# A two-block transformer kernel: another order for the last layers' products and weight splits, and a value projection that moves high and low weights together

## The reference, cut to what matters

```python
proj = xn @ w_in[layer]
sb_q, sb_k, sb_v, r_q, r_k, r_v, r_g = jnp.split(proj, split_at, axis=-1)
```

```python
hm = rmsnorm(x, norm_mlp_g[l])
x = x + jnp.square(jax.nn.relu(hm @ w_up[l])) @ w_down[l]
return rmsnorm(x, norm_final_g)
```

## Time and profile before

| what | value |
|---|---|
| median of 3 runs | 1605.78 us |
| profiled execution | 1605.47 us |
| its span in the trace | 1603.7 us |
| PE busy | 1565.6 us (98%) |
| DVE busy | 983.5 us (61%) |
| ACT busy | 789.0 us (49%) |
| POOL busy | 608.2 us (38%) |
| granted clock of PE, mean | 0.99 |

### The profile page before, as it was taken

How to read it: one execution, slowest core, us unless ns; L and a number is a source line. 1 busy time by engine, 2 the same in 40 slices (tenths; PEclk the granted TensorE clock), 3 DMA queues, 4 the chain that set the end, 5 groups by cost and what they waited for, 6 DMA issues and landing times.

```text
span 1603.7 us, 20315 instructions
## 1 busy us (share of the span) xinstructions
PE 1565.6 (98%) x7628; PEld 1275.3 (80%) x7628; DVE 983.5 (61%) x1217; ACT 789.0 (49%) x925; POOL 608.2 (38%) x245
## 2 busy tenths in 40 slices
PE   9999999999999999999999999999999989898988
PEld 7888888688888888888898688668868868787876
DVE  6366211782465899899875699744434664737374
ACT  5365222334345788878863432964244533333334
POOL 1422454134342232222225555444314445362725
PEclk9999999999999999999999999999999999999998
DMA  5421243222246999999964336002402323050511
GB/s 203 125 73 53 79 145 118 79 79 80 103 149 238 385 419 405 393 390 390 383 246 143 105 104 173 31 27 79 150 35 79 132 80 130 4 206 1 184 40 53
DMA packets 49768, 252.18 MB, mean 157 GB/s; under 512 B 9953, under 2 KB 12769, under 8 KB 23457
## 3 DMA queue, kind: packets, MB, share of 16 engines
q1 hardware_dynamic: 43344, 238.42, 40.4%
q0 software_dynamic: 5184, 8.40, 1.4%
q10 hardware_dynamic: 1168, 4.39, 0.7%
HBM read 235.57 MB, written 16.78 MB: 157 GB/s over the span
## 4 chain that ended last, share of the span: by engine, by line
PE 82%; DVE 6%; ACT 5%; issue 5%; POOL 2%; DMA 1%; POOLq 0%; SPq 0%; DVEq 0%; ACTq 0%
PE psum L232 23%; PE psum L234 23%; PE psum L233 23%; PE psum L2379 2%; ACT unit_hi L2792 1%; ACT f_hi L2864 1%; PE psum L2414 1%; PE psum L1350 1%; PE psum L1072 1%; PE psum L2402 1%; PE psum L2672 1%; POOL w_lo L148 1%; ACT w_hi L142 1%; POOL unit_lo L2797 1%; DVE f_relu L2940 1%
## 5 line engine op out<-in xcount | busy, mean ns | idle before, releaser
L148 POOL TENSOR_TENSOR w_lo<-raw,w_hi 128x2048 fp32r<-128x2048 f32 x62 | 285.5, 4606 | 470.3 <-ACT w_hi L142 435.4
L1368 DVE TENSOR_TENSOR moe_lo<-moe_w,moe_hi 128x2048 fp32r<-128x2048 f32 x100 | 228.3, 2292 | 31.4 <-ACT moe_hi L1358 30.1
L232 PE MATMUL psum<-x_hi,w_hi 128*128 128x512 f32 (+1 forms) x624 | 241.9, 388 | 1.0 <-POOL w_lo L148 1.0
L233 PE MATMUL psum<-x_lo,w_hi 128*128 128x512 f32 (+1 forms) x624 | 239.6, 384 | 0.0
L234 PE MATMUL psum<-x_hi,w_lo 128*128 128x512 f32 (+1 forms) x624 | 239.6, 384 | 0.0
L142 ACT ACTIVATE w_hi<-raw 128x2048 fp32r<-128x2048 f32 x67 | 128.0, 1911 | 208.3 <-PE psum L234 207.8
L2797 POOL TENSOR_TENSOR unit_lo<-mlp_raw,unit_hi 128x2048 fp32r<-128x2048 f32 x32 | 155.3, 4852 | 168.6 <-DVE unit_lo L2797 88.9
L1358 ACT ACTIVATE moe_hi<-moe_w 128x2048 fp32r<-128x2048 f32 x100 | 191.4, 1915 | 28.0 <-PE psum L234 21.6
L232 PEld LDWEIGHTS psum<-x_hi,w_hi 128*128 128x128 f32 x624 | 117.3, 188 | 26.0 <-issue 3.0
L233 PEld LDWEIGHTS psum<-x_lo,w_hi 128*128 128x128 f32 x624 | 117.3, 188 | 23.4 <-issue 0.7
L234 PEld LDWEIGHTS psum<-x_hi,w_lo 128*128 128x128 f32 x624 | 117.2, 188 | 23.1
(11 more groups left out here) (422 smaller groups left out, 3397.3 us busy)
## 6 DMA issues: line engine op xcount, KB each, us to landing
raw<-in_w_dense SPq DMA_DIRECT2D x67, 1024.0 KB, 4.9
...
```

Of the source, the lines that this page charges most:

```text
L148: pool.tensor_tensor(w_lo[c % RING][:, :], raw[c % RING][:, :], w_hi[c % RING][:, :].bitcast(F32), ALU.subtract).then_inc(lo_ready, 1)
L232: pe.matmul(out, lh, rh, start=first, stop=False, **more)
L233: pe.matmul(out, lh, rl, start=False, stop=False, **more)
L1368: dve.tensor_tensor(ring_lo[s][:, :], ring[s][:, :], ring_hi[s % MOE_HI][:, :].bitcast(F32), ALU.subtract).then_inc(moe_low, 1)
```

## The change

It touches two places.

In the value projection, the high and the low weights now lie in one tensor `w_both`, at the same addresses. One step is two matmuls instead of three: `x_hi` against the high and the low weights side by side in 512 columns, and `x_lo` against the high weights in 256 columns, added to the left half. The two halves of the bank are added by VectorE when it reads them (a TENSOR_REDUCE over 512 elements in place of a copy of 256).

In the last layer pair:
- VectorE lowers units 0, 2 and 3 (before: 2 and 3), so GpSimd lowers one unit less in each group.
- Products 2 to 5 are A12, S4, S2, S3 (before: S2, A12, S3, S4), with other banks, raw quarters, add order and rows to match. `weights_1` stands after pair c = 1 (group 0: c = 0), behind the lowering of unit 0. `weights_2` and the lowering of units 2 and 3 follow `parts_low` of c = 3. `weights_3` and `weights_4` follow the first adds.
- ScalarE rounds a pair's combinations (`parts_high`) before the weight unit that stood ahead of it, save in c = 3. In group 0 the rounding of up0's last chunk (`split_hi` of UP0_C + 3) now stands behind `parts_high` of c = 1.
- At the end, rows q = 2, 3 are squared, gained and scaled first.

```diff
-            for kt in range(KT):
-                mm = three_pass(pe, psum[:, 6 if j in SECOND_V else 7, 0:2 * P], x_hi[:, kt, m * P:(m + 1) * P], x_lo[:, kt, m * P:(m + 1) * P],
-                                wh[:, :, kt, :], wl[:, :, kt, :], kt == 0, kt == KT - 1)
+                pe.matmul(psum[:, bank, :], x_hi[:, kt, rows], wb[:, :, :, kt, :], start=kt == 0, stop=kt == KT - 1,
+                          skip_group_check=True)
+                mm = pe.matmul(psum[:, bank, 0:2 * P], x_lo[:, kt, rows], wb[:, 0, :, kt, :], start=False, stop=kt == KT - 1,
+                               skip_group_check=True)
...
-            dve.tensor_copy(ret_v[:, j % 4, 256 * (j // 4):256 * (j // 4) + 256], psum[:, 6 if j in SECOND_V else 7, 0:256])\
-               .then_inc(bank_free, 1)
+            dve.tensor_reduce(ret_v[:, j % 4, 256 * (j // 4):256 * (j // 4) + 256],
+                              psum[:, bank, :].rearrange("p (s n) -> p n s", s=2), AX.X, ALU.add).then_inc(bank_free, 1)
...
-    LOWERED_BY_VECTOR = (2, 3)
+    LOWERED_BY_VECTOR = (0, 2, 3)
...
-        slots.append([a3, a1, a2, a0])
+        slots.append([a2, a3, a1, a0])
...
-    SUM_OF_UNIT = {1: 1, 2: 3, 4: 2, 6: 4}
-    RAW_OF_UNIT = (B11, B11, B11, B21, B12, B22, B11, 0, 1, 2, 3)
+    SUM_OF_UNIT = {1: 1, 4: 2, 5: 3, 6: 4}
+    RAW_OF_UNIT = (B11, B11, B21, B22, B11, B12, B11, 0, 1, 2, 3)
...
                 rectified(g, 2 * c)
-                if c == 2:
-                    weights_1(g)
-                if c == 3:
-                    weights_2(g)
                 rectified(g, 2 * c + 1)
                 sums(g, c)
                 parts_low(g, c)
-                if c == 2:
-                    weights_3(g)
+                if c == (1 if g else 0):
+                    unit_lower(dve, UNITS * g)
+                    weights_1(g)
                 if c == 3:
                     unit_lower(dve, UNITS * g + 2)
+                    weights_2(g)
+                    unit_lower(dve, UNITS * g + 3)
...
-            add(g, 0, BANKS_X, 2, 0, -4)
-            add(g, 1, BANKS_Y, 0, 1, -3)
-            unit_lower(dve, UNITS * g + 3)
-            add(g, 2, BANKS_X, 2, 1, -2)
+            add(g, 1, BANKS_Y, 0, 1, -2)
+            add(g, 0, BANKS_X, 2, 0, -5)
+            add(g, 2, BANKS_Z, 2, 0, 1)
+            weights_3(g)
             weights_4(g)
...
-            product(g, 2, S2, BANKS_X, added=0)
-            product(g, 3, A12, BANKS_Z, begins=True)
-            product(g, 4, S3, BANKS_X, added=2)
-            product(g, 5, S4, BANKS_Y, added=1)
-            product(g, 6, A22, BANKS_X, added=4)
+            product(g, 2, A12, BANKS_Z, begins=True)
+            product(g, 3, S4, BANKS_Y, added=0)
+            product(g, 4, S2, BANKS_X, added=1)
+            product(g, 5, S3, BANKS_X, added=4)
+            product(g, 6, A22, BANKS_X, added=5)
```

More of the change, by code:

```diff
@@ L93, in build @@
     raw = [at(f"raw{b}", 8 * b, [P, CHUNK_COLS]) for b in range(RING)]
-    w_hi = [at(f"w_hi{b}", 16 + 8 * b, [P, CHUNK_COLS], FR) for b in range(RING)]
-    w_lo = [at(f"w_lo{b}", 32 + 8 * b, [P, CHUNK_COLS], FR) for b in range(RING)]
+    w_both = at("w_both", 16, [P, 2, RING, CHUNK_COLS], FR)
+    w_hi, w_lo = ([w_both[:, i, b, :] for b in range(RING)] for i in range(2))
     x_hi = at("x_hi", 48, [P, KT, S], FR)
@@ L693, in ret_v_tile @@
             b, m = j // 4, j % 4
-            wh = w_hi[(V_C + b) % RING][:, :].rearrange("p (m k n) -> p m k n", k=KT, n=P)
-            wl = w_lo[(V_C + b) % RING][:, :].rearrange("p (m k n) -> p m k n", k=KT, n=P)
+            wb = w_both[:, :, (V_C + b) % RING, :].rearrange("p s (m k n) -> p s m k n", k=KT, n=P)
             if m == 0:
@@ L2820, in mlp_sync @@
                 sp.wait_ge(lows_done, ONCE + UNITS * (g - 1) + 4 + k)
[L2821 to L2822 removed]
+                if k < 2:
+                    sp.wait_ge(t_added, ONCE + 4 * (g - 1) + 3 + k)
                 load("up", g, k)
@@ L2837, in mlp_gpsimd @@
         split_lo(pool, UP0_C + 2)
-        unit_lower(pool, 0)
         split_lo(pool, UP0_C + 3)
-        for U in range(1, UNITS * G - 4):
+        for U in range(UNITS * G - 4):
             if U % UNITS not in LOWERED_BY_VECTOR:
@@ L2844, in mlp_gpsimd @@
         pool.wait_ge(gain_landed, ROWS_LANDED + 16)
+        for q in range(2, TB):
+            pool.wait_ge(p_added, done + 7 + q)
+            pool.tensor_tensor(y_rows[q][:, :], res_t[q][:, :], gain_row[:, :], ALU.mult).then_inc(last_gained, 1)
         for q in range(2):
-            pool.wait_ge(p_added, done + 9 + q)
+            pool.wait_ge(p_added, done + 11 + q)
             pool.tensor_tensor(y_rows[q][:, S:D], res_t[q][:, S:D], gain_row[:, S:D], ALU.mult).then_inc(last_gained, 1)
-        for q in range(2, TB):
-            pool.wait_ge(p_added, done + 9 + q)
-            pool.tensor_tensor(y_rows[q][:, :], res_t[q][:, :], gain_row[:, :], ALU.mult).then_inc(last_gained, 1)
     def mlp_scalar(act):
@@ L2873, in mlp_scalar @@
         squares(0, 0)
+        parts_high(0, 0)
         unit_high(act, 0)
-        parts_high(0, 0)
         squares(0, 1)
+        parts_high(0, 1)
         split_hi(act, UP0_C + 3, UP0_T + 4)
-        parts_high(0, 1)
         rows_copied(0)
@@ L2881, in mlp_scalar @@
         squares(0, 2)
+        parts_high(0, 2)
         unit_high(act, 1)
-        parts_high(0, 2)
         rows_copied(2)
@@ L2892, in mlp_scalar @@
                 unit_high(act, U0 - 2)
-                squares(g, 0)
-                unit_high(act, U0 - 1)
-                parts_high(g, 0)
-                for c in range(1, 4):
+                for c in range(3):
                     squares(g, c)
-                    unit_high(act, U0 + c - 1)
                     parts_high(g, c)
+                    unit_high(act, U0 - 1 + c)
+                squares(g, 3)
+                unit_high(act, U0 + 2)
+                parts_high(g, 3)
             for n in range(3, PRODUCTS + 2 * (g + 1 < G)):
@@ L2903, in mlp_scalar @@
         done = 2 * PRODUCTS * (G - 1)
+        for q in range(2, TB):
+            act.wait_ge(p_added, done + 7 + q)
+            act.activation(sq_rows[q % 2][:, :], res_t[q][:, :], ACT.Square, accum_out=row_sum[:, q:q + 1])\
+               .then_inc(last_squared, 1)
+        act.wait_ge(last_squared, COUNTED + 2)
+        act.activation(row_rms[:, 2:TB], row_sum[:, 2:TB], ACT.Sqrt, scale=1.0 / D, bias=col("eps")).then_inc(last_rooted, 1)
         for q in range(2):
-            act.wait_ge(p_added, done + 9 + q)
+            act.wait_ge(p_added, done + 11 + q)
             act.activation(sq_rows[q][:, 0:S], res_t[q][:, S:D], ACT.Square, accum_out=right_sum[:, q:q + 1])\
                .then_inc(last_squared, 1)
+        act.wait_ge(last_inverted, COUNTED + 1)
         for q in range(2, TB):
-            act.wait_ge(p_added, done + 9 + q)
-            act.activation(sq_rows[q % 2][:, :], res_t[q][:, :], ACT.Square, accum_out=row_sum[:, q:q + 1])\
-               .then_inc(last_squared, 1)
-        act.wait_ge(last_squared, COUNTED + TB)
-        act.activation(row_rms[:, 2:TB], row_sum[:, 2:TB], ACT.Sqrt, scale=1.0 / D, bias=col("eps")).then_inc(last_rooted, 1)
-        for q in range(2, TB):
-            act.wait_ge(last_gained, COUNTED + q + 1)
-            act.wait_ge(last_inverted, COUNTED + 1)
+            act.wait_ge(last_gained, COUNTED + q - 1)
             act.activation(y_rows[q][:, :], y_rows[q][:, :], ACT.Copy, scale=row_rstd[:, q:q + 1]).then_inc(last_right, 1)
@@ L3021, in mlp_vector @@
         dve.reciprocal(row_rstd[:, 2:TB], row_rms[:, 2:TB]).then_inc(last_inverted, 1)
+        dve.wait_ge(last_squared, COUNTED + TB)
+        dve.tensor_scalar(right_mean[:, 0:2], right_sum[:, 0:2], 1.0 / D, EPS, ALU.mult, ALU.add).then_inc(last_mean, 1)
         done = 2 * PRODUCTS * (G - 1)
```

26 lines of the change are left out of this document (12 added, 14 removed).

## The result

| | before | after |
|---|---|---|
| median of 4 runs | 1605.43 us | 1582.97 us (1582.57 to 1584.94) |
| profiled execution | 1605.47 us | 1584.94 us |
| its span | 1603.7 us | 1583.1 us |

The ratio is 0.9861, with a 95% interval from 0.9844 to 0.9878. 1582.0 had been forecast, with a range from 1577 to 1589.

A forecast was written before the change was run, and what follows sets the result against it. TensorE, busy 98% of the span, was taken to bound the kernel. Terms of -19.2, -2.3, +0.2, -1.3 and -1.2 sum to -23.8 us: from 1605.47 to 1581.7, with 0.3 for the median 1582.0 us, range 1577 to 1589.

The forecast's parts named there:

- value projection: Value steps: merged matmuls 13.3 ns shorter, -1.7 us over 128 steps; with the longer reading, -1.2 us left.
- group 0, to the start of c = 3: Last layer pair: up0 ends 6.0 us later, c = 3 starts at 1297.9 instead of 1297.68, +0.2 us.
- groups 1 to 3: Last layer pair: stops go, a group takes 82.05 us; 265.34 us between starts of c = 3 becomes 246.15, -19.2 us.
- last 132 matmuls: The 12 of c = 3 and products 2 to 6 at the end: 32.63 us becomes 30.4, -2.3 us.
- the end: After TensorE's end: VectorE's add for q = 1 comes about 0.9 us after it instead of 2.2, -1.3 us.
- The stops ahead of c = 3: TensorE's waits for `f_lo` in each group, about 4.4 us and 2.5 us of lower clock, go in groups 1 to 3.
- T: Moment when TensorE ends the last up tile; `f_lo` of c = 3 forecast at T + 7.0, due at T + 8.16.
- The wait ahead of product 5: Each group: unit 5, lowered by GpSimd, ends at T + 27.6 for T + 27.2, a new wait of 0.45 us.
- The lower clock: Group 0: 2.1 us added for TensorE's slower clock behind the idle ahead of up0's last chunk, which starts 3.9 us late.
- the rivals: Stop stays in part, 1598 us (0.07); slower chain, 1611 (0.05); group 0 and reading cost more, 1588 (0.06); nothing, 1605 (0.02).
- the slower one: Unit 4, `weights_3`, unit 5, product 5: GpSimd slips one pass, product 5 waits 5.1 us, 1611 us; chance 0.05.

The follow-up runs named there:

- the second: The changed kernel once more, unaltered, on one chip beside other kernels: 1583.36 us (1582.03 to 1583.78).
- the last layer pair alone: The changed kernel with the value projection as it was before (three matmuls of 256 columns, a copy): 1585.08 us, ratio 0.9866.
- the early chunk: The changed kernel with up0's last chunk rounded ahead of the high parts of c = 1 in group 0: 1579.49 us, ratio 0.9837; again 1579.46 us.
- the last experiment: The early chunk with the value projection as it was before (three 256-column products, a copy): 1581.31 us against 1579.46.

## Why the prediction was right, and what its terms measured

The spans fell by 20.6 us in the first profile after, by 22.3 in the second. By stretches, in us:

| term | predicted | first profile | second |
|---|---|---|---|
| value projection | -1.2 | -0.5 | -0.5 |
| untouched code ahead of the last pair | 0 | +1.0 | +0.9 |
| group 0, to the start of c = 3 | +0.2 | -0.3 | -1.9 |
| groups 1 to 3 | -19.2 | -18.1 | -18.1 |
| last 132 matmuls | -2.3 | -1.9 | -1.9 |
| the end | -1.3 | -0.8 | -0.8 |
| sum | -23.8 | -20.6 | -22.3 |

Groups 1 to 3 are 1545.18 - 1297.90 = 247.28 us where they were 265.34. Group 0 is counted from the first matmul of up0's third chunk, 1260.65 after and 1260.10 before.

- **The stops ahead of c = 3.** Mechanism and size were right: no idle, clock 1.00, `f_lo` at T + 7.1 for T + 7.0. Undoing a part of the new order brings stops back: 1.1 us for `f_lo` with unit 0 on GpSimd, 3.2 us for unit 1 with `weights_1` late. No run shows how much of the old stop each of the two combinations made.
- **The wait ahead of product 5.** Predicted 0.45 us, measured 0.47 to 0.57. The term was short by 0.3 us a group: the interval to the matmul behind the stop is 0.87 us (1399.10 to 1399.97) and to the next 0.34, so the stop costs 0.87 + 0.34 - 2 x 0.227 = 0.76 us. A standstill of TensorE costs more than its idle: the idle is counted from the end of a matmul that the profile gives 0.39 us, where the next one would have started after 0.227, and the matmul behind the stop takes 0.34 to the next start. That is 0.9 of the 1.1 us missing in groups 1 to 3.
- **Group 0.** The chunk starts 16.45 us after the third chunk where it did 12.64 after: 3.8 us later, for 3.9 predicted. The lower clock was taken at 2.1 us. It cost 12.64 - 11.01 = 1.6 us in the first profile and nothing in the second, which is nearly the whole difference between the two executions (1584.94 and 1583.20 us). This is the term with the largest error. Of seven profiles with this stop of 2.0 to 2.1 us unfilled, two show the lower clock (the changed kernel's first, the last layer pair alone) and five do not. What decides it wasn't found.
- **The end.** The forecast had GpSimd's gain multiplications out of the way. But GpSimd lowered unit 6 until 1569.5, behind unit 5, and only then began them. So the wait that was to go came back: ScalarE's scaling of row block 3 waited for GpSimd, the squares of q = 0 behind it came at 1575.36, and the reciprocal, the scaling and the add for q = 1 follow from them. Half a microsecond of the gain went there. The long `TENSOR_SCALAR` is not on this path, since the add behind it ended 0.5 us before ScalarE came to the squares. With unit 5 off GpSimd, ScalarE scales both row blocks without a wait, the `TENSOR_SCALAR` takes 0.36 us, and the span ends 6.0 us after TensorE's last matmul instead of 7.2.
- **The value projection.** Under half of what was predicted. A step is 353.7 ns for 346.7, which takes 128 x 7 ns = 0.9 us from the 1.7; the head that waits lost 0.2 as foreseen. The step that failed is the one that let the 512-column matmul cost 226.7 ns beside a 256-column one, as in rows where only 512 follow each other. By the fixed cost of 2.5 ns that the Trainium skill gives (TensorE: Matmul & The Clock Gate, the section on 56 ns against 53.3) the merge is worth an estimated 0.3 us. A step shortened by 5.7 ns (359.4 to 353.7), 0.7 us for 128 steps, so the measurement lies between the two.
- **Untouched code.** Nothing was predicted here. In the 14 profiles of this study, the stretch from the end of the stick-breaking stage to up0's third chunk comes in two lengths, with nothing between: 1092.0 to 1092.6 us in 6 (the kernel before and both of the early chunk's among them) or 1093.7 to 1094.2 in 8 (both of the changed kernel's among them). The difference arises at 520 to 600 us, where the experts' weights come in. That stretch, first the changed kernel and then the early chunk's second run:

```profile
520.00:600.00 80.00, 77.25 (x396) 1.00 0.97 394
```

```profile
520.00:600.00 80.00, 78.37 (x403) 1.00 0.98 400
```

ScalarE's waits for those weights from 500 to 700 us, in the same order (total us, times, longest):

```profile
ACT moe_hi L1361 <- DMA moe_w<-in_w_moe: 12.9, 9, 3.8
```

```profile
ACT moe_hi L1361 <- DMA moe_w<-in_w_moe: 5.2, 5, 1.9
```

TensorE does 1.1 us less work there in the first case, with the DMA engines busy throughout. Kernels with the old and with the new projection fall in both classes. That these two lengths also make the two clusters in the timed runs (the early chunk's five: 1579.22, 1579.30, 1579.46, 1580.63, 1581.36) is likely but not shown, since only one run of each kernel has a profile. It fits the 1.9 us of the last experiment: 0.5 of the projection and 1.5 of this.

None of the rivals came true. The nearest was the slower one: its chain is the one that sets product 5's wait, but no pass of GpSimd slipped into it.

The forecast of the total was good by luck as well. The errors of the terms (+0.7, +1.1, +0.4, +0.5 and +0.9 of untouched code) were partly met by the clock that mostly did not fall (-2.1).
